# Sample projections turned feature-major, norm weights from 4 KB loads, longer dummy bursts and new tie numbers in a hybrid encoder layer on eight cores

## The reference

```python
h = RMSNorm(x) * g_pre
u = h @ W_in                      # 1024 x 4096: rq rk rv rg hq hf hi hg, 512 columns each
# group A: retention, 4 heads of 128, rotary q and k, decay gamma_h per head
# group B: HGRN2, 4 heads of 128, q = SiLU(hq), f = lb + (1 - lb) * sigmoid(hf), k = 1 - f, v = hi
# each head: S <- decay * S + k^T v,   o_t = q_t S_t   (causal, state S is 128 x 128)
o = concat(SiLU(rg) * headnorm(o_A), SiLU(hg) * headnorm(o_B))
y = x + RMSNorm(o @ W_out) * g_post
```

## Time and profile before

| | us |
|---|---|
| median of 3 runs (378.22 to 398.82) | 378.24 |
| the profiled execution's own time | 378.07 |
| its span on the slowest core (core 3) | 376.5 |
| spans of the eight cores | 373.7 to 376.5 |

### The profile page before, as it was taken

One profiled execution on the slowest core, in us unless ns is written; L12 is line 12 of the kernel. 1 busy time (PEld: TensorE's weight loads), 2 busy tenths in 40 slices (PEclk: granted clock), 3 DMA queues, 4 the chain that ended last, 5 costly groups with the idle time before them and its releaser, 6 DMA issues.

```text
span 376.5 us, 7940 instructions; the slowest of 8 cores (373.7 to 376.5 us)
## 1 busy us (share of the span) xinstructions
PE 357.6 (95%) x2343; PEld 188.3 (50%) x2343; DVE 234.8 (62%) x524; ACT 183.5 (49%) x567; POOL 218.5 (58%) x292
## 2 busy tenths in 40 slices
PE   7789799999999999999999999999999999999992
PEld 8554354445554445454545454545455455545541
DVE  0237454995958868658684858666657466458445
ACT  2251244868858746263636262626262534544651
POOL 8425531775668765848565667375647455454640
PEclk9989799999999999999999999999999999999997
DMA  7999999999521979653958346362393464465407
GB/s 175 208 174 165 176 165 205 238 220 181 100 71 17 264 116 254 146 138 78 144 131 200 67 77 142 105 110 83 69 120 69 123 98 127 76 144 134 170 9 190
DMA packets 60619, 51.56 MB, mean 137 GB/s; under 512 B 41632, under 2 KB 48832, under 8 KB 60576
## 3 DMA queue, kind: packets, MB, share of 16 engines
q1 hardware_dynamic: 53104, 32.69, 35.5%
q0 software_dynamic: 7472, 18.35, 32.6%
HBM read 41.73 MB, written 10.09 MB: 138 GB/s over the span
## 4 chain that ended last, share of the span: by engine, by line
PE 78%; DMA 10%; DVE 4%; POOL 3%; ACT 2%; issue 2%; DVEq 0%; POOLq 0%; ACTq 0%
PE bank L732 44%; PE bank L715 15%; PE bank L1010 12%; DMA Wi<-w_in 10%; PE bank L928 2%; PE bank L933 2%; PE bank L945 1%; PE bank L896 1%; ACT og L956 1%; POOL Wi L604 1%; POOL rsq L963 1%; DVE fR L786 1%; PE bank L997 1%; DVE Sst L950 1%; DVE xs L950 1%
## 5 line engine op out<-in xcount | busy, mean ns | idle before, releaser
L732 PE MATMUL bank<-Wi,xT 128*128 128x512 bf16 (+1 forms) x816 | 190.5, 383 | 4.3 <-DMA Wi<-w_in 3.2
L732 PEld LDWEIGHTS bank<-Wi,xT 128*128 128x128 bf16 (+1 forms) x816 | 78.1, 99 | 91.2 <-issue 9.2
L966 DVE SCALAR_TENSOR_TENSOR og<-bank,rsq,gate 128x128 bf16<-128x128 f32 (+1 forms) x136 | 38.8, 343 | 39.9 <-POOL rsq L963 36.5
L1010 PE MATMUL bank<-Wo,ogT 128*128 128x512 bf16 (+1 forms) x272 | 62.1, 379 | 0.2
L715 PE MATMUL bank<-xT,Wi 128*128 128x512 bf16 (+1 forms) x320 | 61.9, 340 | 0.4 <-DVE AT L904 0.3
L885 POOL TENSOR_TENSOR Sst<-Sst,decS 128x512 f32<-128x512 f32 x30 | 32.1, 1078 | 18.4 <-DVE Sst L950 13.0
L715 PEld LDWEIGHTS bank<-xT,Wi 128*128 128x128 bf16 x320 | 26.7, 97 | 31.3 <-issue 3.4
L1010 PEld LDWEIGHTS bank<-Wo,ogT 128*128 128x128 bf16 (+1 forms) x272 | 25.9, 98 | 29.7 <-issue 0.8
L963 POOL TENSOR_TENSOR rsq<-ssq,mhalf 128x4 f32<-128x4 f32 (+1 forms) x34 | 34.5, 1018 | 4.6 <-POOL ssq L960 0.4
L782 POOL TENSOR_TENSOR KTh<-fG 128x512 bf16<-128x512 f32 (+1 forms) x20 | 17.5, 877 | 33.4 <-DVE fG L774 31.7
L956 ACT ACTIVATE og<-bank 128x128 bf16<-128x128 f32 (+1 forms) x136 | 35.6, 287 | 1.7 <-PE bank L933 1.5
(11 more groups left out here) (99 smaller groups left out, 460.6 us busy)
## 6 DMA issues: line engine op xcount, KB each, us to landing
xr<-xp POOLq DMA_DIRECT2D x15, 512.0 KB, 6.0
yp<-xr SPq DMA_DIRECT2D x15, 512.0 KB, 3.3
xs<-xp SPq DMA_DIRECT2D x12, 512.0 KB, 6.6
Wi<-w_in POOLq DMA_DIRECT2D x6, 1024.0 KB, 47.0
xr<-xp SPq DMA_DIRECT2D x5, 512.0 KB, 14.1
Wi<-w_in POOLq DMA_DIRECT2D x4, 512.0 KB, 20.3
Wo<-w_out POOLq DMA_DIRECT2D x2, 1024.0 KB, 80.1
rot<-rot_p SPq DMA_DIRECT2D x16, 96.0 KB, 6.4
```

Of the source, the lines that this page charges most:

```text
L732: ins = e.matmul(pb(v)[0:L, :], lhsT=k.xT[:, kc, j * 128:j * 128 + L], rhs=Wi[:, kc, seg * 512:(seg + 1) * 512], start=(kc == 0), stop=(kc ...
L966: S.op(DVE, lambda e, q_=q_, h=h, vo=vo: e.scalar_tensor_tensor(out=ogs[vs][0:L, h * 128:(h + 1) * 128], in0=pb(vo)[0:L, q_ * 128:(q_ + 1) ...
L1010: ins = e.matmul(pb(y)[0:L, :], lhsT=ogT[:, kc, 0:L], rhs=Wo[:, kc, n * 512:(n + 1) * 512], start=(kc == 0), stop=(kc == 7))
```

## The change

- The sample's values and gates are projected feature-major: for each of four segments and each of its four chunks of 128 columns, the weights are stationary and `xT`'s 48 columns stream (128 matmuls in all). The result [128 features, 4 x 48] is scaled (DVE, by a new table `tkf`) or copied or put through SiLU (ACT) into `vgT`, transposed back by PE (4 per segment) and copied by ACT into `V` or `gate`.
- `g_pre` and `g_post` are loaded as 8 rows of 128 floats, split into three bf16 parts on ACT and DVE, spread over 128 partitions by 48 matmuls against a selection built from the identity, and copied from PSUM by ACT and DVE. These loads and the steps of g_pre have the highest boost on their engines.
- A burst of dummies is as long as 0.6 of the time to the next step (6 at least).
- `S.slack` falls from 3000 to 2000, and the random numbers come from 29 pieces, each with a seed, an amplitude and a stretch of the operations.
- The cost table counts a POOL load whose last axis is 512 at 1.13 of its bytes.

```diff
+                        if e == POOL and name == "dma_start" and out.shape[-1] == 512:
+                            nbytes = int(nbytes * 1.13)
...
-            noise = np.random.RandomState(self.jitter[0]).uniform(-1.0, 1.0, n) * self.jitter[1]
-            for i in range(n):
-                prio[i] += float(noise[i])
+            for seed_, amp_, a_, b_ in self.jitter:
+                noise = np.random.RandomState(seed_).uniform(-1.0, 1.0, n) * amp_
+                for i in range(int(a_ * n), int(b_ * n)):
+                    prio[i] += float(noise[i])
...
-                    put(burst, {dep_op} | set(bk[2]), bk[1])
-                    for d in reversed(chain[1:]):
-                        put(burst, {dep_op, d} | set(bk[2]), bk[1])
+                    steps = chain[:0:-1]
+                    at = [prev_fin] + [done_at(d) for d in steps] + [o["t_start"]]
+                    for q, d in enumerate([None] + steps):
+                        cnt = max(burst, int(0.6 * (at[q + 1] - at[q]) / fdur))
+                        put(cnt, {dep_op} | set(bk[2]) | (set() if d is None else {d}), bk[1])
...
-        gid = S.op(SP, lambda e: e.dma_start(out=gpre[:], in_=g_pre), writes=["gpre"], dma_key="gpre")
-        S.ops[gid]["boost"] = 19.5e6
-        late_dma.append(S.op(SP, lambda e: e.dma_start(out=gpost[:], in_=g_post), writes=["gpost"], dma_key="gpost"))
+        sel, g8, res, part = AT[0:8, :, :], Sst_p[0:8, 0:256], Sst_p[0:8, 256:512], ogT
+        n0 = len(S.ops)
+        for v, src in enumerate((g_pre, g_post)):
+            S.op(SP, lambda e, v=v, src=src: e.dma_start(out=g8[:, v * 128:(v + 1) * 128], in_=src), writes=[("g8", v)], dma_key=("g8", v))
+        S.op(DVE, lambda e: e.tensor_copy(out=sel, in_=ident[0:8, 0:8].unsqueeze(2).to_broadcast([8, 8, 128])),
+             reads=["ident"], writes=[("AT", 0), ("AT", 1)])
...
+        S.op(ACT, lambda e: e.activation(out=p2[0], in_=g8, func=AF.Copy), reads=G8, writes=["ogT"])
+        S.op(DVE, lambda e: e.tensor_tensor(out=res, in0=g8, in1=p2[0], op=ALU.subtract), reads=G8 + ["ogT"], writes=["S0"])
...
+        for v, dst, key in ((0, gpre, "gpre"), (1, gpost, "gpost")):
+            for n in range(2):
+                T = S.bank()
+
+                def bc(e, v=v, n=n, T=T):
+                    ins = None
+                    for q in range(4):
+                        for i in range(3):
+                            ins = e.matmul(pb(T)[:, q * 128:(q + 1) * 128], lhsT=sel[:, n * 4 + q, :], rhs=part[0:8, 2 * i + v, :],
+                                           start=(i == 0), stop=(i == 2))
+                    return ins
+                S.op(PE, bc, reads=["ogT", ("AT", 0), ("AT", 1)], writes=[T])
...
+            if k.sample:
+                for n, (seg, kind, off) in enumerate(((2, "v", 0), (6, "v", 512), (3, "g", 0), (7, "g", 512))):
...
+                        for c in range(4):
+                            for kc in range(8):
+                                ins = e.matmul(pb(v)[:, c * L:(c + 1) * L], lhsT=Wi[:, kc, seg * 512 + c * 128:seg * 512 + (c + 1) * 128],
+                                               rhs=k.xT[:, kc, 0:L], start=(kc == 0), stop=(kc == 7))
...
+                    if seg == 2:
+                        S.op(DVE, lambda e, v=v, n=n: e.tensor_tensor(out=vgT[:, n, :], in0=pb(v)[:, 0:4 * L], in1=tkF[:, :], op=ALU.mult),
+                             reads=[v, "tkF"], writes=[("vgT", n)])
+                    else:
+                        S.op(ACT, lambda e, v=v, n=n, kind=kind: e.activation(out=vgT[:, n, :], in_=pb(v)[:, 0:4 * L],
+                                                                             func=AF.Copy if kind == "v" else AF.Silu),
+                             reads=[v], writes=[("vgT", n)])
...
+                        for c in range(4):
+                            ins = e.transpose(out=pbb(T)[0:L, c * 128:(c + 1) * 128], in_=vgT[:, n, c * L:(c + 1) * L], identity=ident[:])
...
+                    S.op(ACT, lambda e, T=T, dst=dst, off=off: e.activation(out=dst[0:L, off:off + 512], in_=pbb(T)[0:L, 0:512], func=AF.Copy),
+                         reads=[T], writes=[(nm, sl, off)])
+                return
...
-        S.slack = 3000.0
-        S.jitter = (10, 500.0)
+        S.slack = 2000.0
...
-        m["g_pre"] = np.ascontiguousarray(np.broadcast_to(g_pre, (128, D_MODEL)))
-        m["g_post"] = np.ascontiguousarray(np.broadcast_to(g_post.reshape(1, D_MODEL), (128, D_MODEL)))
+        m["g_pre"] = np.ascontiguousarray(g_pre.reshape(8, 128))
+        m["g_post"] = np.ascontiguousarray(g_post.reshape(8, 128))
```

More of the change, by code:

```diff
@@ L507, in build_nc @@
     w_out = din("w_out", [1024, 1024])
-    g_pre = din("g_pre", [128, 1024])
-    g_post = din("g_post", [128, 1024])
+    g_pre = din("g_pre", [8, 128])
+    g_post = din("g_post", [8, 128])
     lbs = din("lbs", [128, 8])
@@ L513, in build_nc @@
     tk = din("tk", [128, 2, 12])
+    tkf = din("tkf", [128, 192])
     gl = din("gl", [128, 2, 4])
@@ L586, in build_nc @@
         late_dma = []
+        vgT = sb("vgT", [128, 4, 4 * LS], BF16)
+        tkF = sb("tkF", [128, 4 * LS], F32)
         warm = sb("warm", [128, 1], F32)
@@ new lines, in build_nc @@
+        S.op(DVE, lambda e: e.tensor_copy(out=sel, in_=ident[0:8, 0:8].unsqueeze(2).to_broadcast([8, 8, 128])),
+             reads=["ident"], writes=[("AT", 0), ("AT", 1)])
+        G8 = [("g8", 0), ("g8", 1)]
+        p2 = [part[0:8, 2 * i:2 * i + 2, :].rearrange("p a b -> p (a b)") for i in range(3)]
+        S.op(ACT, lambda e: e.activation(out=p2[0], in_=g8, func=AF.Copy), reads=G8, writes=["ogT"])
+        S.op(DVE, lambda e: e.tensor_tensor(out=res, in0=g8, in1=p2[0], op=ALU.subtract), reads=G8 + ["ogT"], writes=["S0"])
@@ new lines, in build_nc @@
+        S.op(ACT, lambda e: e.activation(out=p2[1], in_=res, func=AF.Copy), reads=["S0"], writes=["ogT"])
+        S.op(DVE, lambda e: e.tensor_tensor(out=p2[2], in0=res, in1=p2[1], op=ALU.subtract), reads=["S0", "ogT"], writes=["ogT"])
+        for v, dst, key in ((0, gpre, "gpre"), (1, gpost, "gpost")):
[9 more added lines that the diff above has]
+                S.op(PE, bc, reads=["ogT", ("AT", 0), ("AT", 1)], writes=[T])
+                S.op(ACT if n == 0 else DVE, (lambda e, dst=dst, T=T: e.activation(out=dst[:, 0:512], in_=pb(T)[:, :], func=AF.Copy)) if n == 0 else
+                     (lambda e, dst=dst, T=T: e.tensor_copy(out=dst[:, 512:1024], in_=pb(T)[:, :])), reads=[T, "S0"], writes=[(key, n)])
+            if v == 0:
+                for i, o in enumerate(S.ops[n0:]):
+                    o["boost"] = 25e6 - 1e4 * i
@@ L622, in build_nc @@
         S.op(SP, lambda e: e.dma_start(out=tkT[:], in_=tk), writes=["tk"], dma_key="tk")
+        tkf_load = lambda: S.op(SP, lambda e: e.dma_start(out=tkF[:], in_=tkf), writes=["tkF"], dma_key="tkF", deps=[sc0[0]])
         S.op(SP, lambda e: e.dma_start(out=glT[:], in_=gl), writes=["glT"], dma_key="glT")
@@ L681, in stage_A @@
                                                        in1=gpre[0:L, :], op0=ALU.mult, op1=ALU.mult),
-                 reads=[xkey, ("rsx", sq), "gpre"], writes=[("xbf", slot)])
+                 reads=[xkey, ("rsx", sq), ("gpre", 0), ("gpre", 1)], writes=[("xbf", slot)])
             if i == 3:
@@ L842, in stage_C, with mm, tr @@
             L = k.rows
+            if k.sample:
+                for n, (seg, kind, off) in enumerate(((2, "v", 0), (6, "v", 512), (3, "g", 0), (7, "g", 512))):
+                    dst, nm = (V[sl], "V") if kind == "v" else (gate[sl], "gate")
+                    v = S.bank(reserve=RESP)
+                    def mm(e, v=v, seg=seg):
+                        ins = None
+                        for c in range(4):
+                            for kc in range(8):
+                                ins = e.matmul(pb(v)[:, c * L:(c + 1) * L], lhsT=Wi[:, kc, seg * 512 + c * 128:seg * 512 + (c + 1) * 128],
+                                               rhs=k.xT[:, kc, 0:L], start=(kc == 0), stop=(kc == 7))
+                        return ins
+                    S.op(PE, mm, reads=WK(seg) + [("xT", k.par, j)], writes=[v, ("vgT", n), (nm, sl, off)])
+                    if seg == 2:
[5 more added lines that the diff above has]
+                             reads=[v], writes=[("vgT", n)])
+                    T = S.bank()
+                    def tr(e, T=T, n=n):
+                        ins = None
+                        for c in range(4):
+                            ins = e.transpose(out=pbb(T)[0:L, c * 128:(c + 1) * 128], in_=vgT[:, n, c * L:(c + 1) * L], identity=ident[:])
+                        return ins
+                    S.op(PE, tr, reads=[("vgT", n), "ident"], writes=[T])
+                    S.op(ACT, lambda e, T=T, dst=dst, off=off: e.activation(out=dst[0:L, off:off + 512], in_=pbb(T)[0:L, 0:512], func=AF.Copy),
+                         reads=[T], writes=[(nm, sl, off)])
+                return
```

(6 more changed lines are left out.)

3 lines of the change are left out of this document (2 added, 1 removed).

## The result

The changed kernel takes 373.46 and 373.71 us where the kernel before takes 378.22 to 378.58: a ratio of 0.9874, 95% interval 0.9845 to 0.9903. Three more executions of it, at 399 to 438 us, ran at a lower granted clock on some cores (0.82 to 0.95) and are left out, like one of the kernel before at 398.82. A second batch gave 374.8 beside 379.3, ratio 0.9889 (0.9871 to 0.9908). So it is faster, by some 4.5 us, and by less than 2%. The forecast was 372.8, and the range of 369.0 to 377.0 held. The sum came out near although several of its terms did not; they were wrong in opposite directions.

A forecast was written before the change was run, and what follows sets the result against it. The start was taken as bound by bytes and all later stages by PE. The terms summed as 378.07 - 1.2 - 2.2 - 2.0 + 0.5 - 0.4 = 372.8 us, with a range of 369.0 to 377.0.

The forecast's parts named there:

- Loads (-1.2): Start: without the two 512 KB norm-weight loads, later Wi loads land earlier; -1.2 us, bounds 0 to -2.6.
- Dummies (-2.2): Ahead of tile 2's transposes: 37 dummies instead of 12 prevent the clock's fall after 41 us; -2.2 us, bounds 0 and -2.4.
- Rival 1: Start: the clock falls all the same on some core, so the 2.2 us are gone; 375.0 us, chance 0.18.
- Late x tiles (+0.5): Block 1: PE arrives sooner but its x tiles move by only 1.2, so PE waits; +0.5 us, between 0 and some 1.5.
- Sample (-2.0): Sample's value and gate projections: 128 matmuls of 48 columns plus transposes replace 32 of 512 columns; -2.0 us.
- Rival 5: Sample's projections: weight loads bind at 97 ns each, +7.0 us for -2.0, so 381.8 us; chance 0.02.
- rival 2: Tail: the sample's 2.0 us stay there, in waits for hand-overs between ACT, POOL and PE; 374.8 us, chance 0.10.
- Tail order (-0.4): End: the second half of the sample's x is queued ahead of two stores, so DVE's wait shrinks; -0.4 us.
- Tie numbers (0): Every stage: new random numbers and the slack of 2000 move work everywhere else; taken as 0.
- rival 3: Every stage: the new order also takes away PE waits, six of 0.46 us, 2.8 in all; 370.0 us, chance 0.14.
- Rival 4: State updates: new order sets consumers too close behind producers, 32 waits of 0.3 us; slower, 382.4 us, chance 0.04.
- The forecast's own case: Whole kernel: all terms hold together; 372.8 us, own range 371 to 374.5, chance 0.52.

The follow-up runs named there:

- run 11: The changed kernel with one more load of 480 KB between the first two x tiles, where the old norm-weight load stood: 376.18 us, 0.9942 of the kernel before.
- run 9: The changed kernel with bursts of 6 dummies again, no other instruction moved: 375.67 us, 0.9932 of the kernel before.
- run 10: The kernel before with the longer dummy bursts alone: 378.53 us beside 379.32, ratio 0.9985.
- run 6: The changed kernel with the sample's values and gates projected token-major again, random numbers kept with their operations: 377.94 us, 1.0000 of the kernel before.
- run 7: The kernel before with the sample's feature-major values and gates alone, random numbers kept with their operations: 382.30 us, ratio 1.0079.
- run 2: The changed kernel with the old slack of 3000 and the one old random pattern instead of the 29 pieces: 382.68 us, 1.0115 of the kernel before.
- run 3: The kernel before with one other seed of its random numbers, 11 for 10, and nothing else: 388.16 us, ratio 1.0236.
- run 4: The changed kernel without the ten random-number pieces of the last 15% of operations, slack of 2000 kept: 381.56 us beside 379.76, 1.0047 of the kernel before.
- run 5: The changed kernel with only the ten tail pieces of random numbers, the 19 earlier left out, slack of 2000 kept: 385.07 us, 1.0146 of the kernel before.
- run 8: The kernel before with the sample's feature-major values and gates, plus dummies in three tail waits: 380.45 us beside 379.72, ratio 1.0022.

## Why the prediction was right, and where it was not

**Loads (-1.2): mis-sized a little.** The price of the bytes was right: 480 KB put the landing off by 1.25 in run 11. But the second quarter's landing moved by 0.8 in the median of the cores (1.2 on the slowest), because SP's two small loads put off the first x tile: it is issued at 1.92 instead of 1.07. I had named these issues and then taken 1.2 all the same. What I did not see is who is late next: POOL. Timeline of core 5:

```profile
40.28 1.39 PE L1199 MATMUL bank<-ident 128*128 128x128 bf16 x22 [0.65 <-DVE tA L842]
...
41.38 1.27 POOL L855 TENSOR_TENSOR Ktr<-tA,tB 128x512 bf16<-128x512 f32 x1
...
42.80 0.38 PE L870 MATMUL bank<-ident,qtm 128*128 128x128 bf16 x4 [1.12 <-POOL Ktr L855]
```

The load landed at 42.36, the rotated k was ready at 42.65 (41.38 + 1.27): the wait that PE had for Wi at 43.78 in the earlier trace rows is now one for POOL. The 22 dummies end at 41.67, a microsecond later than I had it, but still before it.

**Dummies (-2.2): the mechanism was right, the size was not.** The longer bursts take the fall near 42 away, and in run 9 it is back on every core. Rival 1 came true on one core (core 1, clock 0.76 from 41 to 48) without deciding the end. But little of the gain lasts: run 10 gives 0.6, and of run 9's 1.6 to 2.2 about 0.6 stand at the 1200th matmul, the rest being clock lost in the tail. What the term lacked is that a gain at the start is in good part a loan against the x tiles of block 1. The eight spans do not lie within a microsecond either, but 2.2 apart.

**Late x tiles (+0.5): right.** PE's late starts (beyond 0.216 us after a 512-column matmul and 0.055 after one of 128) sum to 1.89 between 60 and 100 us, against 1.44 before. With the two terms above, my start came to -2.9; the table shows 2.8 at the 104th matmul, but only 2.0 at the 200th on core 5 and 0.8 on core 3.

**Sample (-2.0): the price was right, but not all of it reached the end.** 128 matmuls take 3.3 us, where my sum had 3.2. Rival 5 is out: 95 ns are shown for each weight load, and yet a matmul starts every 25 to 27. By the rule of the Trainium skill ("TensorE: Matmul & The Clock Gate", LDWEIGHTS (loading the stationary operand)) the estimate was 13.7; the trace disagrees with it again. At full clock the tail, the sample and its new order together, won 1.3 of the 2.0. The rest is rival 2: the tail waits for POOL, ACT and DVE where PE's columns used to stand. On core 5, which ends last, PE's end gained nothing on its 1200th matmul (5.1, then 5.0), since the half clock took 1.7. Core 3 has the same waits of 0.49 and 0.41 ahead of its last matmuls and keeps its clock; what decides on which core it falls stays open. Runs 6 and 7 show that "what the sample is worth" has no answer by itself: 4.5 in the new order, -3.0 in the old one. Two causes are shown: an order is worth its time only with the list and the tail that it was picked for (runs 2 to 5), and an idle PE near the end can lose the clock for its last 16 matmuls (runs 7 and 8).

**Tail order (-0.4): about right at DVE, and lost behind it.** DVE's last step follows POOL's last at 366.97 - 366.73 = 0.24, against 372.12 - 371.59 = 0.53 before: -0.3. But from the end of that step to the end of the span it now takes 3.5 us, on core 5 as on the others, where it took 2.9 to 3.2. So from the end of W_out to the end of the span nothing is won: 7.2, against 7.1 to 7.3 before. Why the stretch of the last stores grew is not shown.

**Tie numbers (0): the step that failed.** I took them as 0, and against rival 3 I wrote that "no kind of wait comes more than twice". Between 100 and 340 us the list of waits held 1.2 us, these two beside the 0.6 of the earlier trace rows:

```profile
PE bank L896 <- DVE fR L786: 0.3, 1, 0.3
PE bank L715 <- DVE AT L904: 0.3, 1, 0.3
```

PE's late starts, summed as above, held 3.7. They fell to 0.8, and that is the gain between the 200th and the 1200th matmul in the table, 3.1: rival 3 had the size (2.8). That stretch takes 247.4 to 247.5 us on all six cores with complete records before and 244.3 to 245.3 in two profiles of the changed kernel. It is back at 247.7 to 247.9 with the old numbers (run 2) and at 248.0 to 248.9 without the early pieces (run 5; in both, 0.2 of it are short matmuls that stand earlier), and stays at 244.3 to 244.8 with them (run 4). So the gain in the middle belongs to the 19 early pieces, and not to the slack. The list counts an engine as busy until its last matmul has run through the array, so it shows only part of a late start. The larger truth is in runs 2 to 5. Any new list of operations shuffles which number falls to which operation, and the three orders here that nobody picked for their list (runs 2, 3 and 5) cost 9 to 10 us. So the numbers were worth about 9: with the old ones and the old slack the other edits together end 4.4 us slower than the kernel before (run 2), with the picked ones 4.5 faster. Rival 4's sign was a real possibility, by the tail rather than by 32 small waits.

In sum, on core 5: -2.9 for the start was -2.0 (at the 200th matmul), 0 for the middle was -3.1 (at the 1200th), and -2.4 for the tail was +0.5 (the lead of 5.1 became 4.6); a core that keeps its clock in the tail wins 1.2 there. That the total lay 0.8 from the forecast is luck: a start and a tail that gave less (rival 2) and a middle that gave more (rival 3) cancel each other. The forecast's own case, with 0.52, is not what happened.

## What to carry to other kernels

Where a scheduler breaks ties by picked numbers, an edit can't be priced without its order: change the order alone first (one other seed), and hold every edit against that spread. Sum PE's late starts from start to start of its matmuls rather than the waits in the list, and compare two kernels at counts where the same work lies behind them. And when an edit takes columns off PE ahead of a chain of short hand-overs, look at the clock of what follows, on every core: the columns may have been what kept it up.
